# Prompt queries and keys turned in 32x32 blocks on VectorE and gathered from a DRAM scratch, in place of TensorE transposes

## The reference, cut to what matters

```python
h = rms_norm(x, norm_g)                          # x: 1024 prompt rows + 64 sample rows, D_MODEL = 1024
z = einsum('bsd,de->bse', h, w_in)               # q, k, v of A (3 groups of 512) and B (512), and the gates
qa, ka = rms_norm(qa, q_norm_a), rms_norm(ka, k_norm_a)    # over each head of 64
qb, kb = rms_norm(qb, q_norm_b), rms_norm(kb, k_norm_b)
o_a = combine_groups(dilated_window_prompt(qa, ka, va, window, dilation) for 3 groups)
o_b = diff_attention_prompt(qb, kb, vb)          # scores q.k / 8, two softmax maps per head
new caches: k and v rows of prompt and sample, and the old caches moved up by 8 rows
y = x + (sigmoid gates * projections of o_a, o_b) @ w_out
```

## Time and profile before

| | us |
|---|---|
| runs of the kernel before | 1697.97, 1710.6, 1716.54 |
| median | 1710.6 |
| span of the profiled execution, first to last instruction | 1708.6 |
| TensorE busy, weight loads busy | 1633.6 (96%), 1402.9 (82%) |
| VectorE, ScalarE, GpSimd busy | 719.3 (42%), 600.1 (35%), 664.0 (39%) |
| TensorE's share of the chain that ended last | 89% |
| share of 16 DMA engines: SP's queue, ScalarE's queue | 39.9%, 19.7% |

### The profile page before, as it was taken

How to read it: one execution, slowest core, us unless ns; L and a number is a source line. 1 busy time by engine, 2 the same in 40 slices (tenths; PEclk the granted TensorE clock), 3 DMA queues, 4 the chain that set the end, 5 groups by cost and what they waited for, 6 DMA issues and landing times.

```text
span 1708.6 us, 37775 instructions
## 1 busy us (share of the span) xinstructions
PE 1633.6 (96%) x14872; PEld 1402.9 (82%) x14872; DVE 719.3 (42%) x1788; ACT 600.1 (35%) x1405; POOL 664.0 (39%) x958
## 2 busy tenths in 40 slices
PE   7999999999999999999999899999899899999998
PEld 5788677888899999999999877778777787878787
DVE  6521576221472222722226544445354342588511
ACT  5421576222362222722217233334333243422300
POOL 5566120567334565445656111222121111466500
PEclk9999999999999999999999999999999999999999
DMA  5174811766417567156432889889889886865422
GB/s 166 53 238 147 264 43 34 238 209 211 148 44 222 198 226 249 51 185 226 142 105 65 306 264 299 296 305 318 269 296 313 280 276 203 281 210 170 151 93 80
DMA packets 184064, 336.30 MB, mean 197 GB/s; under 512 B 29969, under 2 KB 74130, under 8 KB 177746
## 3 DMA queue, kind: packets, MB, share of 16 engines
q1 hardware_dynamic: 143586, 221.68, 39.9%
q10 hardware_dynamic: 40304, 112.22, 19.7%
HBM read 294.05 MB, written 127.07 MB: 246 GB/s over the span
## 4 chain that ended last, share of the span: by engine, by line
PE 89%; issue 3%; DMA 2%; DVE 2%; ACT 2%; SPq 1%; POOL 1%; ACTq 0%; DVEq 0%; POOLq 0%
PE ps L2004 14%; PE ps L2006 14%; PE ps L2005 14%; PE ps L2056 5%; PE ps L2057 5%; PE ps L2058 5%; PE ps L2213 4%; PE ps L2157 4%; PE ps L2103 3%; PE ps L2177 3%; PE ps L2272 3%; PE ps L2164 2%; PE ps L2255 2%; PE ps L1973 2%; PE ps L2124 2%
## 5 line engine op out<-in xcount | busy, mean ns | idle before, releaser
L989 POOL TENSOR_TENSOR w_lo<-raw,w_hi 128x512 fp32r<-128x512 f32 x140 | 180.6, 1296 | 428.5 <-ACT w_hi L1199 427.9
L2004 PE MATMUL ps<-w_hi,hT 128*128 128x512 f32 x824 | 340.8, 414 | 2.1 <-POOL hT L976 1.0
L2006 PE MATMUL ps<-w_hi,hT 128*128 128x512 f32 x824 | 330.2, 401 | 0.0
L2005 PE MATMUL ps<-w_lo,hT 128*128 128x512 f32 x824 | 330.0, 400 | 0.0
L2056 PE MATMUL ps<-w_hi,hT 128*128 128x256 f32 x768 | 222.3, 289 | 1.5 <-issue 1.1
L2004 PEld LDWEIGHTS ps<-w_hi,hT 128*128 128x128 f32 x824 | 206.0, 250 | 21.3 <-issue 1.4
L2006 PEld LDWEIGHTS ps<-w_hi,hT 128*128 128x128 f32 x824 | 206.2, 250 | 20.5
L2005 PEld LDWEIGHTS ps<-w_lo,hT 128*128 128x128 f32 x824 | 206.7, 251 | 18.0
L2057 PE MATMUL ps<-w_lo,hT 128*128 128x256 f32 x768 | 217.5, 283 | 3.4 <-issue 3.4
L2058 PE MATMUL ps<-w_hi,hT 128*128 128x256 f32 x768 | 216.8, 282 | 0.0
L1199 ACT ACTIVATE w_hi<-raw 128x512 fp32r<-128x512 f32 x158 | 98.9, 629 | 206.6 <-DMA raw<-in_w_in 189.6
(11 more groups left out here) (233 smaller groups left out, 2851.4 us busy)
## 6 DMA issues: line engine op xcount, KB each, us to landing
out<-in_cache_a_kv ACTq DMA_DIRECT2D x29, 2040.0 KB, 9.4
k_in<-in_cache_b_kv SPq DMA_DIRECT2D x128, 256.0 KB, 3.7
v_in<-in_cache_b_kv SPq DMA_DIRECT2D x128, 256.0 KB, 6.1
raw<-in_w_in SPq DMA_DIRECT2D x104, 256.0 KB, 4.0
k_in<-in_cache_a_kv SPq DMA_DIRECT2D x104, 256.0 KB, 7.0
v_in<-in_cache_a_kv SPq DMA_DIRECT2D x104, 256.0 KB, 6.8
out<-in_cache_a_kv ACTq DMA_DIRECT2D x7, 2016.0 KB, 8.9
raw<-in_w_in ACTq DMA_DIRECT2D x40, 256.0 KB, 6.0
```

The costliest lines, as they stand in the source:

```text
L989: pool.tensor_tensor(lo, raw_of(q), hi.bitcast(F32), ALU.subtract).then_inc(lo_done, 1)
L2004: pe.matmul(z, hi, wh, start=first, stop=False)
L2005: pe.matmul(z, hi, wl, start=False, stop=False)
L2006: return pe.matmul(z, lo, wh, start=False, stop=last)
```

## The change

TensorE's `turn` and ScalarE's `move` go, but for the sample tile of the queries. In their place:

- VectorE turns each 128x512 prompt tile in 32x32 blocks (one instruction): of queries in `zn` in place, right after the scaling; of keys from `kn` into `zn`, one tile behind, after the scaling of the next tile.
- SP stores the turned tile to a DRAM scratch (`store_blocks`, 256 KB). VectorE's next scaling into the same half of `zn` waits for this store to land.
- SP gathers the scratch back (`load_turned`) in 16 parts a block, each 32 partitions of 32 pieces of 128 bytes: `qT` in tiles 1 to 8 of the k block (two parts each, after the store of the key tile), `kT` in tiles 1 to 6 of the v block (three parts each).
- `pad_first` waits for the 16 query parts, TensorE's attention for the 16 key parts.
- The query scale is applied by GpSimd in the padding of `qz`, in place of a multiplication by 1.0; the loop of `pad_queries` for group 0 is unrolled. Some semaphores are merged.

```diff
+            def store_blocks(G, kind, i):
+                sp.wait_ge(turned, tile_turned(G, kind, i))
+                sp.dma_start(blocks_scr[G][kind == "k"][i * P:(i + 1) * P, :], zn[:, mi(G, kind, i) % 2, :])\
+                    .then_inc(blocks_sent(G, kind, i)[0], 16)
+
+            def load_turned(G, kind, part):
+                c, j = divmod(part, 4)
+                if part == 0:
+                    for i in range(NT - 2, NT):
+                        sp.wait_ge(*blocks_sent(G, kind, i))
+                    if kind == "q" and G:
+                        sp.wait_ge(o_out, stored(G - 1))
+                base = blocks_scr[G][kind == "k"][0:1, 0:1]
+                src = bass.AP(base.tensor, base.offset + c * P + 32 * j, [[CW, 32], [32 * CW, SEQ // 32], [1, 32]])
+                out = (kT if kind == "k" else qT)[32 * j:32 * j + 32, c * SEQ:(c + 1) * SEQ]
+                sp.dma_start(out.rearrange("p (b r) -> p b r", r=32), src).then_inc(kt_in if kind == "k" else qt_in, 16)
...
                     if i < KC:
                         load_chunk(u + 1, i)
+                    if kind in "qk" and i:
+                        store_blocks(G, kind, i - 1)
+                    if kind == "k" and i:
+                        for part in range(2 * i - 2, 2 * i):
+                            load_turned(G, "q", part)
+                    if kind == "v" and 0 < i < 7:
+                        for part in range(3 * i - 3, min(3 * i, 16)):
+                            load_turned(G, "k", part)
...
-            def copied(out, in_):
-                return pool.tensor_scalar(out, in_, 1.0, None, ALU.mult)
+            def scaled(G, half, i, c):
+                rows, cols = slice(HD * half, HD * half + HD), slice(i * P, (i + 1) * P)
+                return pool.tensor_scalar(qz[rows, half, cols], qT[rows, c * SEQ + i * P:c * SEQ + (i + 1) * P],
+                                          qcol[rows, (0 if G else 1):(0 if G else 1) + 1], None, ALU.mult)
...
-                pool.wait_ge(t_moved, 17 * G + 9)
+                pool.wait_ge(setup, 1)
+                pool.wait_ge(qt_in, 256 * (G + 1))
...
                         if m >= 2:
                             G2, m2 = divmod(m - 2, 18)
-                            if m2 < 9:
-                                dve.wait_ge(t_ready, ti(G2, "q", m2) + 1)
+                            if m2 % 9 < NT:
+                                dve.wait_ge(*blocks_sent(G2, "qk"[m2 // 9], m2 % 9))
+                            elif m2 < 9:
+                                dve.wait_ge(t_ready, G2 + 1)
                             else:
-                                dve.wait_ge(kn_ready, TILES * G2 + m2 - 9 + 1)
+                                dve.wait_ge(kn_ready, TILES * G2 + NT + 1)
                         dve.tensor_tensor(zn[0:r, m % 2, :].rearrange("p (h d) -> p h d", h=8),
...
+                        if kind == "q" and i < NT:
+                            dve.wait_ge(zn_ready, m + 1)
+                            dve.transpose(zn[:, m % 2, :], zn[:, m % 2, :]).then_inc(turned, 1)
+                        if kind == "k" and i:
+                            kk = TILES * G + i - 1
+                            dve.wait_ge(kn_ready, kk + 1)
+                            dve.transpose(zn[:, (m - 1) % 2, :], kn[:, kk % 3, :]).then_inc(turned, 1)
...
-                    if kind == "q" and i:
-                        turn(G, "q", i - 1)
-                    if kind == "k" and i != 1:
-                        turn(G, "q", NT) if i == 0 else turn(G, "k", i - 2)
-                    if kind == "v" and i == 0:
-                        turn(G, "k", NT - 1)
+                    if kind == "k" and i == 0:
+                        turn_sample(G)
...
                 pe.wait_ge(v_ready, 9 * G + 8)
-                pe.wait_ge(t_moved, 17 * G + 17)
+                pe.wait_ge(t_moved, G + 1)
+                pe.wait_ge(kt_in, 256 * (G + 1))
                 attention_a(G) if G else attention_b()
```

More of the change, by code:

```diff
@@ L316, in build_step @@
         st_scr = [dram(f"st_scr{g}", [SEQ, 16]) for g in range(3)]
+        blocks_scr = [[dram(f"blocks_scr{g}{kind}", [SEQ, CW]) for kind in "qk"] for g in range(4)]
         os_scr = dram("os_scr", [2, DEC_B, ROW_C, P])
@@ L337, in build_step @@
         t_ready, t_moved = sem("t_ready"), sem("t_moved")
+        turned = sem("blocks_turned")
+        turn_out = [sem(f"blocks_out{s}") for s in range(2)]
+        qt_in, kt_in = sem("qT_in"), sem("kT_in")
         k_out = [sem(f"k_out{s}") for s in range(3)]
@@ L381, in build_step @@
         m_ready, m_t, m_hi, m_lo = sem("m_ready"), sem("m_t"), sem("m_hi"), sem("m_lo")
-        xl_in = [sem(f"xl_in{s}") for s in range(2)]
+        X_LOADS = [16 * len(range(s, TILES, 2)) for s in range(2)]
         yo_ready = sem("yo_ready")
@@ L393, in mi, with tile_turned, blocks_sent @@
             return 18 * G + (9 if kind == "k" else 0) + i
-        def ti(G, kind, i):
-            return 17 * G + (9 if kind == "k" else 0) + i
+        def tile_turned(G, kind, i):
+            return 16 * G + (8 if kind == "k" else 0) + i + 1
+        def blocks_sent(G, kind, i):
+            m = mi(G, kind, i)
+            return turn_out[m % 2], 16 * sum(x % 18 % 9 < NT for x in range(m % 2, m + 1, 2))
         def x_bank(j):
@@ L1039, in block_ @@
                         split_lo(u + 1, i)
-            def copied(out, in_):
-                return pool.tensor_scalar(out, in_, 1.0, None, ALU.mult)
+            def scaled(G, half, i, c):
+                rows, cols = slice(HD * half, HD * half + HD), slice(i * P, (i + 1) * P)
+                return pool.tensor_scalar(qz[rows, half, cols], qT[rows, c * SEQ + i * P:c * SEQ + (i + 1) * P],
+                                          qcol[rows, (0 if G else 1):(0 if G else 1) + 1], None, ALU.mult)
             def pad_first(G):
-                pool.wait_ge(t_ready, 17 * G + 17)
+                pool.wait_ge(turned, tile_turned(G, "k", NT - 1))
+                for i in range(NT - 2, NT):
+                    pool.wait_ge(*blocks_sent(G, "k", i))
                 for s in range(3):
@@ L1958, in _, with turn_sample @@
                     turn_x(i, half)
-            def turn(G, kind, i):
-                t, r = ti(G, kind, i), nrows(i)
-                if kind == "q":
-                    pe.wait_ge(zn_ready, mi(G, "q", i) + 1)
-                    src = zn[0:r, mi(G, "q", i) % 2, :]
-                else:
-                    kk = TILES * G + i
-                    pe.wait_ge(kn_ready, kk + 1)
-                    src = kn[0:r, kk % 3, :]
-                if t >= 2:
-                    pe.wait_ge(t_moved, t - 1)
+            def turn_sample(G):
+                m = mi(G, "q", NT)
+                pe.wait_ge(zn_ready, m + 1)
                 for c in range(NC):
-                    ins = pe.transpose(bank(3 + t % 2)[:, c * P:c * P + r], src[:, c * P:(c + 1) * P],
-                                       ident[0:r, 0:r])
+                    ins = pe.transpose(bank(3)[:, c * P:c * P + NS], zn[0:NS, m % 2, c * P:(c + 1) * P],
+                                       ident[0:NS, 0:NS])
                 ins.then_inc(t_ready, 1)
```

78 lines of the change are left out of this document (27 added, 51 removed).

## The result

| | before | after |
|---|---|---|
| median of the runs, us | 1713.57 (4 runs, 1697.97 to 1719.49) | 1758.44 (4 runs, 1753.82 to 1766.74) |
| span of the profiled execution, us | 1708.6 | 1753.5 |
| mean granted clock of TensorE | 0.991 | 0.973 |

The ratio is 1.028, with an interval of 1.025 to 1.032: the changed kernel is slower by 44.9 us, where 19 had been forecast. 1758 lies in the range given (1686 to 1785) and outside the forecast's own one (1718 to 1750).

A forecast was written before the change was run, and what follows sets the result against it. TensorE was taken to set the time in the blocks around the change. Terms of -27 + 40 + 6 = +19 us on the 1708.6 us span gave 1727.6, with 2.0 for the median 1730 us; range 1686 to 1785.

The forecast's parts named there:

- the 27 us of the turns: Query and key blocks: 64 TensorE turns of 0.42 us go, all on the path, 27 us gained.
- The two loops of the key block: Key blocks: scaling waits for the store from zn, and weight chunks queue behind stores and gathers; 40 us lost.
- Query blocks "hidden": Query blocks: same store, but the loop has two tiles, 11.2 us, for 1.4 + 6.3, so no cost.
- The value block: Attention waits for all 16 key gathers: 3 us each in groups 1 and 2, 6 us; 0 in groups 0 and 3.
- A gather was priced as engine work: Gathers on SP's queue: 1.3 us of the DMA engines each, bounds 0.33 and 2.7 us.
- The count of engine-us: Value blocks of groups 1 and 2: 21 us of gathers added to 37 us, 58 us in 49 and 50.
- the copies can slip: Value blocks: copies may end after the block, so 3 us each was taken, nearer the lower end of 0 to 9.
- Rival C: Gathers are the bound at 2.7 us each, 90 us more in key blocks, a third absorbed: 1790 us; chance 0.11.
- Rival A: Key blocks: stores mostly miss the copies, leaving only late chunks, up to 2 us a block: 1692 us; chance 0.22.
- B: Gain and loss cancel: 20 of 46 us of lateness caught up by each block's 7 us slack: 1710 us; chance 0.27.
- Nothing for the attentions and for what comes after: Attentions and everything after the four groups: a change of 0 us.
- What was said to show it: Key blocks of groups 0 to 2: zn waits for blocks_scr, ScalarE for raw, TensorE idles at the end, DMA share near 1.0.

The follow-up runs named there:

- experiment 3: Changed kernel with turned keys in their own buffer (1762.13 us), key-block weight chunks issued two tiles earlier (1740.8 us), or both (1714.63 us).
- buffer_ahead: Changed kernel with turned keys in a buffer of their own and weight chunks issued two tiles earlier in key blocks: 1714.63 us, ratio 1.0009.
- experiment 4: Ten cache copies moved from value blocks of groups 1 and 2 to the following attentions: changed kernel 1735.7 us; on top of buffer_ahead 1690.88 us.
- nocopy_after: Changed kernel with all 48 cache copies left out: 1671.32 us, ratio 0.9759.
- v_moved: Changed kernel with the ten cache copies of the value blocks of groups 1 and 2 issued in the attentions that follow: 1735.7 us, ratio 1.0136.
- nocopy_before: Kernel before the change with all 48 cache copies left out: 1715.3 us, ratio 1.0018.
- moved_before: Kernel before the change with its copies moved out of key and value blocks into query blocks and attentions: 1726.28 us, ratio 1.0076.
- ba_v_moved: buffer_ahead with the ten copies of the value blocks of groups 1 and 2 issued in the attentions that follow: 1690.88 us, ratio 0.988.
- moved: Changed kernel with all copies out of key and value blocks, 15 in query blocks of groups 1 to 3, 33 in attentions: 1690.69 us, ratio 0.987.
- spread: Changed kernel with both edits of buffer_ahead; copies: 15 in query blocks, 12 in key blocks, the rest in attentions of groups 0 to 2: 1675.54 us, ratio 0.9811.

## Why the prediction was half right

**Where TensorE is the bound, and the 27 us of the turns: right.** The query blocks are 12.0 us shorter (13.5 forecast), the key and value blocks without copies 16.6 (13.5).

**The two loops of the key block: right in mechanism, in place and nearly in time and size.** The scalings at 98.94, 115.53 and 132.90 stand within 1.4 us of the steps worked out, and the late chunks are the second half, as experiment 3 shows. The term was 40 us, 15/11/9/5 by group. Key and value blocks are late by 60.4 us, 19.0/13.5/20.5/7.4. The two loops account for 46.9 of it, near the 40 predicted; the other 13.5, in groups 0 and 2, stay when both loops are open. No run tried their cause, but the trace of `buffer_ahead` shows where they arise. In group 0 SP is held for 7.04 us in issuing two gathers of queries beside a copy, asks for the last weight chunk only at 123.67, and that lands after 9.3 us: TensorE stands 4.70 us for `w_lo`. In group 2's key block TensorE stands 1.52 and 2.94 us, at a granted clock of 0.94 over the block; that belongs to the query block, below.

**Query blocks "hidden": right for `zn`, wrong for the weights.** In the last tiles of group 2's query block the new store stands before the chunk, and both beside two copies. The chunk issued at 594.78 lands after 13.5 us, where the one of the kernel before, issued at 556.55, took 6.0; ScalarE idles 6.77 us for it, the sample queries are scaled late, and TensorE stands 2.92 us for them at 614.37. The key block that follows takes 55.4 us, where without copies it takes 50.2. The prediction had no term for it, and the edits of `buffer_ahead` do not touch it (14.3 us for that chunk there).

**The value block: this is the step that failed.** "Between 0 and 9 us each; I take 3 each" was 16.3 and 8.5 us measured, four times the term and with one group outside its bounds, and 22.7 us of the median by experiment 4. The place was right in the main: the last key gathers are the whole of the wait in group 2 and all but 2.9 us of it in group 1. The price was wrong. A gather was priced as engine work, 1.3 us, to be added to the copies' share, and that number is near the truth where no copy runs. In `buffer_ahead`, in the stretch 440 to 444, between two copies, the queue's pieces take 64 x 0.889 / 3156 = 0.018 us each, with some larger ones of a weight chunk among them, so at most 1.15 us for the 64 of a gather, and a gather lands in 4.2 us:

```profile
q1 hardware_dynamic: 3156, 0.64, 88.9%
...
kT<-blocks_scr1k SPq DMA_DIRECT2D x4, 128.0 KB, 4.2
```

Beside a copy it has no such price: its pieces wait for one large piece each, and the queue, with all behind it, nearly stands still for as long as copies run. The count of engine-us (37 + 21 = 58 in 49) couldn't see this, since it takes the order of service for free. And "the copies can slip", the reason for the lower end, did not help: they ran while the last gathers were due. The prediction had no wait for ScalarE's half sample tile behind the split of chunk 7; that is the 2.9 us. Rival C ("the gathers are the bound, 2.7 us each") had both of its signs, a gather of 18.9 us and TensorE idle before the scores, and too plain a mechanism: three gathers in line hold SP for 4.53 us without copies (`nocopy_after`, 399.21) and the kernel is fast, and for 16.90 us beside them.

**Rival A and B.** A fell: the stores meet the copies in each of the three cases in group 0. B wanted 20 of 46 us caught up; the lateness that was left, 60.4 and 24.8, is more than the 46 before any catching up.

**Nothing for the attentions and for what comes after: two errors that partly cancel.** The attentions of groups 1 and 2 took 64.7 and 55.2 us, 62.2 and 51.9 before. All after them took 16.3 us less. The same stretches of the kernel before, with the granted clock in the last column but two:

```profile
449.30:511.50 62.20, 62.19 (x452) 56.59 (x453) 45.99 (x192) 40.86 (x154) 25.20 (x48) 1.00 0.16 44
672.50:724.40 51.90, 50.16 (x389) 46.67 (x388) 39.45 (x193) 37.79 (x153) 25.19 (x48) 1.00 0.23 71
929.70:1708.60 778.90, 724.73 (x10204) 608.41 (x10202) 348.08 (x729) 237.23 (x432) 209.94 (x385) 0.98 0.73 243
```

The clock is 0.96 and 0.92 in the two attentions after the waits where it was 1.00, and in `v_moved`, without the waits, they take 62.2 and 51.9 us again. Padding with the query scale takes 609 ns an operation (L1074; 525 before), 256 times, and TensorE seldom waits for it: 0, as said.

**What was said to show it.** zn waiting for blocks_scr, ScalarE waiting longer for raw, TensorE idle in the first value tiles: all there. The DMA share "near 1.0" was not in the key blocks (0.71 to 0.78) but in the value blocks (0.94, 0.97), which is where the loss was.

## What to carry to other kernels

Price a DMA of many small pieces by what shares the engines with it, not by its own engine time: beside a queue of large pieces each small one waits for a large one, and everything behind it on the same queue, and behind that on the other engines, waits too. Before a stream of such transfers is put on a queue, list what stands behind it and keep loads with a due time ahead of it, or keep the large transfers out of the same stretch. When one wait is taken away and the time stays, look for a second one of about the same length before dropping the theory: here each of two loops was worth 0 to 18 us alone and 44 together.

## What the runs showed of the hardware that was not expected

- The two queues are served piece by piece in turn: 108 pieces of 10.9 KB and 108 of 128 bytes in the same 4 us.
- A stall costs more than its length. After the 6.21 us at 133.65, TensorE's matmuls follow each other every 0.43 us until about 137, then every 0.23 (the timeline of TensorE above): the lower of its two clocks, 1.2 GHz, before 2.4 again. The granted clock over the value blocks of groups 0 to 2 is 0.90, 0.92 and 0.89, and the busy time of those of groups 1 and 2 grew from 48.74 and 50.00 us to 52.59 and 53.70. The Trainium skill, "TensorE: Matmul & The Clock Gate", Part 1, has the clock halved when the engine has not been busy enough, and the trace agrees; the prediction counted stalls by their length alone.
- After the attentions, where the code is the same, every kernel with the change took 760.5 to 772.3 us, and the kernel before, `nocopy_before` and `moved_before` took 776.0 to 782.1. Of the 16.3 us between the two lines above, 5.8 are busy time of TensorE and 10.5 idle time. Why was not tried, and stays open; in the three pairs with the copies alike it makes the change look 3.7 (no copies), 14.2 (moved) and 16.3 us better than its own parts would.
- The same instructions can meet the copies otherwise. The key block of group 1 took 55.4 to 55.8 us in `v_moved`, `ba_v_moved`, `moved` and `spread`, 50.8 in the changed kernel and 49.5 in `buffer_ahead`, though up to its end `v_moved` and the changed kernel have the same instructions. The last weight chunk of the query block ahead of it, asked for beside two copies, landed after 12.9 to 13.1 us in the four, and after 8.4 and 4.7 us in the other two; in `moved` TensorE then stood 3.04 us for the sample queries, as in group 2 above, and the granted clock over the key block was 0.94. What makes the two copies run side by side with the chunk was not tried; it is the likeliest place for more.
